# Memory rows turned during the second feed-forward, memory projections right behind its last product, x transposed between their layers

## The reference

```
x = x + g_f * swiglu(h, w_gate_up[1], w_down[1])     # last line of the first block
...
mem_kv = mem @ w_mem_kv[layer]                       # second block, for layer 0 and 1
h = x @ a_w_in[0]                                    # input projection of its layer 0
```

## Time and profile before

| | |
|---|---|
| median of 3 runs | 1527.23 us (1525.97 to 1529.92) |
| span of the profiled execution | 1531.1 us, 3.9 us above that median |
| PE busy | 1393.8 us, 91% of the span |
| DVE busy | 1043.8 us, 68% |
| ACT busy | 763.9 us, 50% |
| POOL busy | 86.0 us, 6% |
| last down product of the second feed-forward ends | about 716.4 us |
| input projection's first product starts | 759.88 us |

### The profile page before, as it was taken

One profiled execution on the slowest core, in us unless ns is written; L12 is line 12 of the kernel. 1 busy time (PEld: TensorE's weight loads), 2 busy tenths in 40 slices (PEclk: granted clock), 3 DMA queues, 4 the chain that ended last, 5 costly groups with the idle time before them and its releaser, 6 DMA issues.

```text
span 1531.1 us, 19757 instructions
## 1 busy us (share of the span) xinstructions
PE 1393.8 (91%) x7546; PEld 1191.3 (78%) x7546; DVE 1043.8 (68%) x1068; ACT 763.9 (50%) x745; POOL 86.0 (6%) x80
## 2 busy tenths in 40 slices
PE   5996999999999899998898689999998978999995
PEld 5975778887899788886898577788877967787884
DVE  7685678877675574454435757888884465788886
ACT  2665344433333434332336326677773484577773
POOL 0010000000100000000000010400003000300000
PEclk9998899999899999999899898999998999799998
DMA  9984559997574375555344212799993621299991
GB/s 359 378 297 143 165 193 302 305 311 261 185 253 140 122 236 192 171 185 165 124 144 145 83 43 83 225 339 352 347 332 111 229 74 56 89 318 346 350 353 55
DMA packets 205898, 327.68 MB, mean 214 GB/s; under 512 B 9520, under 2 KB 140272, under 8 KB 205824
## 3 DMA queue, kind: packets, MB, share of 16 engines
q1 hardware_dynamic: 192528, 276.71, 53.6%
q0 software_dynamic: 13296, 49.93, 9.8%
HBM read 325.56 MB, written 1.05 MB: 213 GB/s over the span
## 4 chain that ended last, share of the span: by engine, by line
PE 74%; DVE 15%; ACT 6%; issue 2%; DMA 2%; SPq 0%; DVEq 0%; ACTq 0%
PE ps L1996 22%; PE ps L1997 21%; PE ps L1998 21%; DVE w_low L1231 4%; ACT w_high L644 2%; PE ps L2489 1%; PE ps L2583 1%; PE ps L2262 1%; PE ps L2176 1%; DMA raw<-in_w_qkv 1%; DVE stats L1727 1%; DVE h_low L1881 1%; DVE scratch L1655 1%; DVE x_rows L1718 1%; PE ps L2189 1%
## 5 line engine op out<-in xcount | busy, mean ns | idle before, releaser
L1231 DVE TENSOR_TENSOR w_low<-raw,w_high 128x2048 fp32r<-128x2048 f32 (+1 forms) x256 | 588.0, 2303 | 311.3 <-ACT w_high L644 309.3
L644 ACT ACTIVATE w_high<-raw 128x2048 fp32r<-128x2048 f32 (+1 forms) x256 | 484.1, 1894 | 373.6 <-PE ps L1998 346.4
L1996 PE MATMUL ps<-w_high,h_high 128*128 128x512 f32 (+1 forms) x928 | 364.4, 393 | 11.4 <-DVE h_low L1387 4.0
L1997 PE MATMUL ps<-w_low,h_high 128*128 128x512 f32 (+1 forms) x928 | 357.9, 386 | 0.0
L1998 PE MATMUL ps<-w_high,h_low 128*128 128x512 f32 (+1 forms) x928 | 357.9, 386 | 0.0
L1996 PEld LDWEIGHTS ps<-w_high,h_high 128*128 128x128 f32 x928 | 176.4, 190 | 46.3 <-issue 7.2
L1998 PEld LDWEIGHTS ps<-w_high,h_low 128*128 128x128 f32 x928 | 176.3, 190 | 35.3
L1997 PEld LDWEIGHTS ps<-w_low,h_high 128*128 128x128 f32 x928 | 176.6, 190 | 32.6 <-issue 0.2
L1996 PE MATMUL ps<-h_high,w_high 128*128 128x256 f32 x624 | 183.3, 294 | 16.2 <-DVE h_low L1324 10.6
L1997 PE MATMUL ps<-h_low,w_high 128*128 128x256 f32 x624 | 181.7, 291 | 0.0
L1998 PE MATMUL ps<-h_high,w_low 128*128 128x256 f32 x624 | 181.5, 291 | 0.0
(11 more groups left out here) (319 smaller groups left out, 1411.1 us busy)
## 6 DMA issues: line engine op xcount, KB each, us to landing
raw<-in_w_down SPq DMA_DIRECT2D x124, 512.0 KB, 4.8
raw<-in_w_gate_up SPq DMA_DIRECT2D x88, 512.0 KB, 5.0
scratch<-in_w_ada POOLq DMA_DIRECT2D x40, 1024.0 KB, 5.6
raw<-in_w_gate SPq DMA_DIRECT2D x80, 512.0 KB, 5.1
raw<-in_w_up SPq DMA_DIRECT2D x80, 512.0 KB, 6.3
raw<-in_w_qkv SPq DMA_DIRECT2D x24, 512.0 KB, 13.0
raw<-in_w_o SPq DMA_DIRECT2D x24, 512.0 KB, 6.3
raw<-in_w_in SPq DMA_DIRECT2D x24, 512.0 KB, 4.9
```

The source lines that it names most:

```text
L644: act.activation(wh[u % SPL][:, :, 0:w], raw[u % RAW][:, :, 0:w], ACT.Copy).then_inc(h_split, 1)
L1231: dve.tensor_tensor(wl[u % SPL][:, :, 0:w], raw[u % RAW][:, :, 0:w], wh[u % SPL][:, :, 0:w].bitcast(F32), ALU.subtract).then_inc(l_split, 1)
L1996: pe.matmul(o, h1, h2, start=start, stop=False, skip_group_check=True)
L1997: pe.matmul(o, h1, l2, start=False, stop=False, skip_group_check=True)
```

## The change

The memory rows are fetched by POOL during the second feed-forward, as soon as its input is transposed and `rows` is free. In four of its chunks (the third turn's to the sixth's) PE transposes four 128 x 128 blocks of them into bank 3, ACT writes their high part and DVE their low part to two new tensors that lie over `features`. Behind the last `down` the dummy products and the transposes of memory are gone; PE projects memory layer 0, transposes x, projects layer 1, and goes on to the input projection. ACT and DVE follow: DVE splits the third and fourth memory unit before the low parts of x. The loops of the feed-forward are written out for these chunks.

```diff
+            pool.wait_ge(xt_ready, 16)
+            pool.dma_start(tv[:, :, :], A["mem_2"].rearrange("b (t p) d -> p (b t) d", p=P)).then_inc(mem_loaded, 16)
             pool.wait_ge(x_ready, xrd.up(2))
...
-            pool.dma_start(tv[:, :, :], A["mem_2"].rearrange("b (t p) d -> p (b t) d", p=P)).then_inc(mem_loaded, 16)
...
+            def mem_part(g):
+
+                act.wait_ge(mem_turned, mtn.up())
+                act.activation(mem_h[:, 2 * g:2 * g + 2, :], ps[:, 3, :].rearrange("p (k t) -> p k t", k=2), ACT.Copy).then_inc(mem_high, 1)
...
-                loops = (chunks - 1) // 2
+                peeled = 6 if with_mem else 0
+                for c in range(1, 1 + peeled):
+                    chunk(0)
+                    n[0] += 3
+                    if c >= 3:
+                        mem_part(c - 3)
...
             act.wait_ge(x_ready, xrd.up())
-            transposed()
             for l in range(DEPTH):
+                if l:
+                    transposed()
                 chunk_ready("mem", l)
...
             ahead(PLAN["a_in"])
-            transposed()
...
+            def mem_rest(g):
+
+                dve.wait_ge(mem_high, mhi.up())
+                dve.tensor_tensor(mem_l[:, 2 * g:2 * g + 2, :], ps[:, 3, :].rearrange("p (k t) -> p k t", k=2),
+                                  mem_h[:, 2 * g:2 * g + 2, :].bitcast(F32), ALU.subtract).then_inc(mem_low, 1)
...
+                        if r >= 2:
+                            mem_rest(r - 2)
...
+            ahead(PLAN["mem"] + 1)
             transposed_plain()
-            for l in range(DEPTH):
-                ahead(PLAN["mem"] + 2 * l + 1)
+            ahead(PLAN["mem"] + 3)
             ahead(PLAN["a_in"])
-            transposed_plain()
...
+            def mem_turn(g):
+
+                if g:
+                    pe.wait_ge(mem_low, mlo.up())
+                else:
+                    pe.wait_ge(mem_loaded, 16)
+                for k in range(2):
+                    for t in range(TT):
+                        c = (2 * g + k) * P
+                        i = pe.transpose(ps[:, 3, k * S + t * P:k * S + (t + 1) * P], tv[:, t, c:c + P], ident[:, :])
+                i.then_inc(mem_turned, 1)
...
+                peeled = 4 if with_mem else 0
+                for g in range(peeled):
+                    turn()
+                    gate_up(0)
+                    mem_turn(g)
+                    down(2, False, False)
+                    n[0] += 3
...
-            ffn("ffn1", NFF, before_last=lambda: ffn_gate(1))
-            keep_busy(32, 2)
-            pe.wait_ge(x_ready, 4)
-            pe.wait_ge(mem_loaded, 16)
-            transposes(tv)
+            ffn("ffn1", NFF, before_last=lambda: ffn_gate(1), with_mem=True)
+            pe.wait_ge(mod_taken, mtk.up())
+            pe.wait_ge(mem_low, mlo.up())
             for l in range(DEPTH):
+                if l:
+                    pe.wait_ge(x_ready, 4)
+                    transposes(xs)
...
-            transposes(xs)
```

More of the change, by code:

```diff
@@ L116, in build @@
         FT = sb("features", [P, 20, S])
+        features_at = nc.sbuf_base - 20 * S * 4
+        mem_h, mem_l = (nc.alloc_sbuf_tensor_at(name, [P, KT, S], F32R, offset=features_at + i * KT * S * 4)
+                        for i, name in enumerate(("mem_t_high", "mem_t_low")))
         tv = sb("rows", [P, TT, D])
@@ L179, in build @@
         mem_loaded = sem("mem_loaded")
+        mem_turned = sem("mem_turned")
+        mem_high = sem("mem_high")
+        mem_low = sem("mem_low")
         h_split = sem("h_split")
@@ L605, in apply_rows @@
                 pool.wait_ge(x_ready, xrd.up())
-                pool.wait_ge(xt_ready, 4 * turns)
+                pool.wait_ge(xt_ready, 4 * turns - 4)
                 if turns != 8:
@@ L843, in _, with ffn @@
             silr, atr, ahr = Count(sil_ready), Count(at_ready), Count(ah_ready)
-            def ffn(ph, chunks):
+            mtn = Count(mem_turned)
+            def mem_part(g):
+                act.wait_ge(mem_turned, mtn.up())
+                act.activation(mem_h[:, 2 * g:2 * g + 2, :], ps[:, 3, :].rearrange("p (k t) -> p k t", k=2), ACT.Copy).then_inc(mem_high, 1)
+            def ffn(ph, chunks, with_mem=False):
                 def silu():
@@ L870, in ffn @@
                 n[0] += 2
-                loops = (chunks - 1) // 2
+                peeled = 6 if with_mem else 0
[4 more added lines that the diff above has]
+                        mem_part(c - 3)
+                loops = (chunks - 1 - peeled) // 2
                 with looped(act, loops, {hsp: 6, used: 6, silr: 2, atr: 2, ahr: 2}):
@@ L875, in ffn @@
                 n[0] += 6 * loops
-                for _ in range(chunks - 1 - 2 * loops):
+                for _ in range(chunks - 1 - peeled - 2 * loops):
                     chunk(0)
@@ L905, in _ @@
             norm_first(1, 7)
-            ffn("ffn1", NFF)
+            ffn("ffn1", NFF, True)
             ahead(PLAN["mem"])
             act.wait_ge(x_ready, xrd.up())
-            transposed()
             for l in range(DEPTH):
+                if l:
+                    transposed()
                 chunk_ready("mem", l)
@@ L1494, in _ @@
             silr, acr, ahr, asp = Count(sil_ready), Count(act_ready), Count(ah_ready), Count(a_split)
+            mhi = Count(mem_high)
+            def mem_rest(g):
+                dve.wait_ge(mem_high, mhi.up())
+                dve.tensor_tensor(mem_l[:, 2 * g:2 * g + 2, :], ps[:, 3, :].rearrange("p (k t) -> p k t", k=2),
+                                  mem_h[:, 2 * g:2 * g + 2, :].bitcast(F32), ALU.subtract).then_inc(mem_low, 1)
             def ffn(ph, chunks, weight, extra=None, first_extra=None):
@@ L1529, in ffn @@
                 if first_extra:
-                    for r in range(2):
-                        chunk(1 + r, 0, lambda: first_extra(r))
+                    for r in range(6):
+                        chunk(1 + r, 0, (lambda: first_extra(r)) if r < 2 else None)
                         n[0] += 3
-                    peeled = 1
+                        if r >= 2:
+                            mem_rest(r - 2)
+                    peeled = 3
                 per = {hsp: 6, lsp: 6, silr: 2, acr: 4, ahr: 2, asp: 2}
@@ L2020, in bank_of_h, with unit_features @@
                     pe.wait_ge(h_ready, hr.up())
-            def unit_features(u, b0, nb, k0, first, last, fresh=False):
+            def unit_features(u, b0, nb, k0, first, last, fresh=False, x=(hh, hl)):
                 for b in range(nb):
@@ L2241, in _, with ffn @@
             acr, atr, asp = Count(act_ready), Count(at_ready), Count(a_split)
-            def ffn(ph, chunks, fresh=True, before_last=None):
+            mlo = Count(mem_low)
+            def mem_turn(g):
[8 more added lines that the diff above has]
+                i.then_inc(mem_turned, 1)
+            def ffn(ph, chunks, fresh=True, before_last=None, with_mem=False):
                 def gate_up(j, fresh=False):
@@ L2294, in ffn @@
                 n[0] += 3
-                loops, rest = divmod(chunks - 3, 2)
+                peeled = 4 if with_mem else 0
[5 more added lines that the diff above has]
+                    n[0] += 3
+                loops, rest = divmod(chunks - 3 - peeled, 2)
                 with looped(pe, loops, {lsp: 6, used: 6, acr: 4, atr: 2, asp: 2}):
@@ L2354, in _ @@
                     pe.wait_ge(l_split, lsp.up())
-                    unit_features(n[0], pair, 2, UK * q, q == 0, q == 1, l == 0)
+                    unit_features(n[0], pair, 2, UK * q, q == 0, q == 1, x=(mem_h, mem_l))
                     for t in range(TT):
@@ L2359, in _ @@
                             u = n[0]
-                            i = mm3(ps[:, pair + 1, t * S:(t + 1) * S], hh[:, UK * q + k, tok], hl[:, UK * q + k, tok],
+                            i = mm3(ps[:, pair + 1, t * S:(t + 1) * S], mem_h[:, UK * q + k, tok], mem_l[:, UK * q + k, tok],
                                     wh[u % SPL][:, k, 256:512], wl[u % SPL][:, k, 256:512],
```

5 lines of the change are left out of this document (2 added, 3 removed).

## The result

The first timing gave 1513.05 us for the changed kernel (1512.15 to 1516.26, 4 runs) against 1528.58 us (4 runs) for the one before: ratio 0.9897, 95% interval 0.9878 to 0.9917, so 12.7 to 18.6 us faster. The forecast of 1507.9 us and its range to 1512.0 both lie under the median. The profiled execution spans 1510.5 us.

What follows compares the result with a forecast made beforehand. PE time and PE's waits on the chain were taken as the bound. Removed 13.96 + 0.07 + 4.53 + 1.97 = 20.53 us, less 1.2 added, gives 19.3; 1527.2 - 19.3 = 1507.9 us, range of 8 in 10 1504 to 1512.

Steps and rivals of the forecast that it cites:

- first hole: From the last down product to the first memory product, PE waits on x, memory fetch and transposes: 13.96 us removed.
- the level of 1527.2 us: Median time of the kernel before, from which the forecast gain of 19.3 us was subtracted.
- Second hole and its clock: Between memory products and input projection: 4.53 us of waiting removed, plus 1.97 us lost to the slow clock in its first chunk.
- Memory transposes in the chunks: Four groups of 4 transposes in feed-forward chunks 3 to 6: 0.29 us paid each, 1.2 us added.
- Rival 1: Feed-forward chunks: memory transposes paid in full, 0.66 us each time, 2.6 us; kernel at 1509.3 us; chance 0.15.
- rival 3: Feed-forward chunks: ACT's and DVE's added work not hidden, 5.0 us instead of 1.2; kernel at 1511.7 us; chance 0.06.
- rival 2: Behind x's bare transposes the clock falls and products run at half rate: 2.0 us back, 1509.9 us; chance 0.08.
- the rule of the Trainium skill: PE-mode transposes do not count as activity for the clock gate, so x's bare group looks idle to it.
- PE never idle there: In the new order through the projection's first chunk PE has no idle time, so all 1.97 us of slow clock return.
- rivals 4 and 5: Memory rows land late, eating the gain at 600 us, chance 0.02; holes reopen later, about 1526 us, chance 0.03.

## Why the prediction was wrong

The mechanism was right and sizes were off. The steps that failed are the term of 13.96 us for the first hole, which came to 12.3 in the mean of five profiles; the level of 1527.2 us from which I subtracted, which came to 1529.8 over 43 runs; and a fall of the clock ahead of the seam, which the sum left out.

- **First hole: closed as told, but its size is the term that was wrong.** I took 13.96 us from one profile. Over five profiles with the old seam it is 10.6 to 14.5 us, 12.3 in the mean, 1.7 less (0.7 less by the three of before alone): the transfer took 5.1 to 8.0 us, and only behind the long ones did the transposes run at half clock. That the transfer would be as long each time was an assumption that no row bore out; the bounds of the range covered the transposes and not this.
- **Second hole and its clock: right.** The idle time was 4.53 us in every profile of before. The clock behind it cost 1.4 to 2.6 us, in the mean 1.9, where I had 1.97. Undoing this part alone cost 7.2 us in the profile and 8.2 in the medians of 6 runs each, where I had 6.5.
- **The level.** I subtracted 19.3 from 1527.2, the median of the 3 runs I had. The 43 runs of the kernel before that stood beside the kernels of this study have a median of 1529.8 (1523.63 to 1535.79): 2.6 us more. With the 13 further runs of it above it is 1530.2. I had set the profiled execution's 3.9 us over that median aside as its own, though it is as good a sample as the other three. It was even further above: the time of a run is 1.6 to 1.7 us more than its span wherever both are on record, so that execution's 1531.1 stands for some 1532.7, 5.5 over the median.
- **Memory transposes in the chunks: right, a little dear.** 1.2 us forecast, 0.87 measured, with DVE's product as the cover. Rival 1 (paid in full, 2.6) and rival 3 (5.0) fall: chunks of 17.29 and 17.35 us, not 17.7 or 18.3.
- **The clock behind bare transposes: rival 2 falls**, and with it, for this kernel, the rule of the Trainium skill: 64 in a row left PEclk at 1.00.
- **A fall I had not counted.** 1.6 to 1.7 us behind the wait ahead of the last down product, in 2 of 3 profiles of the changed kernel and in 0 of 3 of the one before. I had read "PE never idle there" off the stretch behind the last down product and not looked at the wait ahead of it.
- **Late rows, reopened holes: rivals 4 and 5 fall.** The rows land 26 us before PE asks, and the split comes 5.5 us early. Nothing reopens later: from the 108th split to the end the three profiles of before take 743.9 to 745.7 us, those of the changed kernel 745.0 to 745.4. Ahead of the 72nd split, where both run the same code, executions differ by more: 548.4 to 552.4 before, 547.4 to 549.4 changed.

With the runs of both kernels put together (43 and 16), the medians are 1529.8 and 1511.8 us: 18.0 us. The profiles give 55.62 - 36.49 = 19.1 at the seam, less 0.9 for the chunks, 18.2, less what falls behind the wait cost, on average 1.1 if they come in 2 of 3 executions. So the 5.1 us by which 1507.9 lies under 1513.05 can be put as 2.6 of level, 1.3 of the sum (19.3 against 18.0), and 1.2 by which the first four runs of the changed kernel lie above its 16. That is bookkeeping, not proof: two of the three comparisons (12.5 to 19.9 and 14.5 to 21.4 us faster) hold 19.3 in their intervals, and two sets of runs of one program had medians 3.35 us apart. The terms are shown wrong by the profiles; how much of the missed 5.1 us each made in the runs stays open. I should have given the length of a transfer and the level of three runs their own spread: with 12.3 for the hole and 1529.8 for the level the same sum gives 1529.8 - 17.6 = 1512.2.

## What to carry to other kernels

A hole read from one profile that holds a transfer is a sample of that transfer, and here the long samples had a fall of the clock in them too: look at the same kind of transfer elsewhere, or give the hole the spread, before its whole length goes into a sum. Subtract from as many runs as there are, and from the profiled execution too. When a hole behind a step closes, look at the wait ahead of that step next: there independent work of the following stage gained another 4.4 us in the profile and 5.0 in the medians.

## What the runs showed of the hardware

One program's executions on one chip lay over 14 us (1523.66 to 1537.37, 12 runs), nearly 1%; their mean granted clock went from 0.952 to 0.965, and profiles differed in which waits were followed by a stretch at the lower of the two levels (1.2 GHz; PEclk 0.57 and 0.62 over windows of 4 us that hold one), at 1.6 to 1.7 us of PE time each. A wait of 2.51 us on PE was followed by such a stretch in 7 of 12 profiles, a filled one in none of 2. A transfer of 1 MB by POOL with no other one beside it took 5.1 to 8.0 us over five executions. PEclk stayed at 1.00 over 7 us in which PE had nothing but fp32 transposes.
